# A hybrid decoder layer on one core: the first tiles' splits and square adds put on VectorE, token tile 0 reordered, attention started two sub-tiles later

## The chip, the cores and the metric

One Trainium2 chip, one of its cores. The metric is the device time of one execution of the whole program, in microseconds. Matrix products run on TensorE (PE), elementwise work on VectorE (DVE), ScalarE (ACT) and GpSimd (POOL); transfers are issued from the queues of SyncE (SP) and ScalarE. Each engine takes its instructions in program order, and the engines wait for one another by semaphores.

## What is computed

One layer, for a prompt of 1024 tokens and 8 decoding sequences of 8 tokens: 1088 tokens of 1024 channels in float32. Cut to what matters:

```python
xn = x * rsqrt(mean(x * x) + 1e-6) * g_pre
qa, ka, va, za, qm, km, vm, om, zm, ig, fg = split(xn @ w_in)
a_out = sliding_window_attention(qa, ka, va, sinks) * silu(za)   # window 128, ALiBi
h, C, n, m = mlstm(qm, km / sqrt(128), vm, ig, log_sigmoid(fg))  # chunks of 128
m_out = sigmoid(om) * rms(h, g_mh) * silu(zm)
y = concat(a_out, m_out) @ w_out
return x + rms(y, g_post), new caches, C, n, m
```

## The kernel before

Every float32 operand of a large product is split into a rounded high part and the rest, the low part, and a product is three passes: high by high, and the two mixed ones. The channels make 8 blocks, counted by kk. The 1088 tokens are cut into three sub-tiles of 368, 368 and 352 columns (SUBS); a weight tile has 128 columns of w_in, and there are 25 of them in the order ka, qa, km, qm, za, om, zm. Sub-tiles are numbered through, three to a tile: tile 5, the first of km, begins with sub-tile 15 (S_KM), and za with sub-tile 39 (S_P3).

**First tiles.** Weight tiles 0 and 1 are computed while x arrives (first_tiles, line 518). For each kk, VectorE casts the weights' high part (first_hi, 1139), GpSimd subtracts it for the low part (line 1560), ScalarE makes x's high part (862) and its square (867), and VectorE x's low part (x_lo, 1145), which PE needs for its third pass. The squares are summed in two chains: VectorE adds the odd ones (add_squares, 1154), GpSimd squares 4 and 6 into a second sum (1564), and a last add of VectorE joins the two. PE turns the sum into one column for each token tile (square_sums, 528), VectorE makes mean squares of it (1164, 1165), GpSimd raises them to the power of minus one half (1546), and PE spreads the result over partitions by nine transposes (spread_rstd, 538).

**Token tiles.** The values and gates are computed with tokens on partitions, nine tiles of 48 products each (two halves q; 324 columns), from a weight whose high part ScalarE makes in four pieces (936) and whose low part VectorE makes in four (wt_lo_part, 1159). In token tile 0 the three products of one kk stand together, each pair of blocks waits for VectorE's piece, and the transposes stand behind the fifth block. On VectorE all four pieces come before the mean squares. ScalarE copies the tile out (883), and behind it each tile of x is scaled by its rstd.

**Projections.** project() makes the other tiles, 24 products a sub-tile (590), into two PSUM banks in turn; ScalarE's evac() copies a sub-tile out (928) and, at places listed in PLAN, makes the high part of a coming weight tile (split_hi, 903); GpSimd or VectorE make the low part (split_lo, 343). Weights arrive through two buffers: load_w(n) on SP (374) waits until tile n-2 has been split. The order of SP's queue is written out by hand: loads 2 and 3, row resets, token outputs, attention biases, value bands (395, 397), two copies of old cache entries (399), loads 4 and 5, row outputs (404 to 406), and then a loop from load 6 on with the transfers of the later stages between.

**Rows and attention.** Between sub-tile 6 and 14 VectorE works out the gates' running sums and maxima as rows (1238 to 1265); PE transposes them (618) ahead of sub-tile 15, and ScalarE, behind its evacuation of sub-tile 15, takes the exponentials of these columns (967). Attention begins with sub-tile S_P2 = 16: in each iteration PE does one unit's scores (638), one sub-tile, and in every second one the values of a block (664). There are 17 units, and 23 iterations up to sub-tile 38. The first scores wait for ScalarE's exponentials (cols_done). The end of the attention gives out the keys (SP 432, 433), and only then do the first state loads (414) and weight load 14 go out; sub-tile 39 begins the mLSTM stage.

## Time and profile before

| | us |
|---|---|
| median of 3 runs | 569.39 |
| lowest and highest | 569.07, 569.61 |
| the profiled execution | 567.94 |
| its span, first to last instruction | 566.1 |
| mean granted clock of TensorE in it | 0.991 |

Times in rows count from the start of the span. In a row of the timeline the first number is the start, the second the time from the first start to the last end of the instructions merged (xN); what stands in brackets is the idle time before it and who ended it. PE's products overlap, so their durations are longer than their spacing. In the chain of waits each piece of time belongs to the work that ended last. The granted clock is a share of full speed.

### The profile page before, as it was taken

The page shows a single profiled execution, that of the slowest core. Times are in us where ns is not written, and L with a number is a line of the kernel's source. Part 1 is how long each engine was busy: PE and PEld are TensorE (multiplying, and loading weights), DVE is VectorE, ACT ScalarE, POOL GpSimd, SP SyncE. Part 2 cuts the span into 40 slices and gives each one's busy share as a digit, 9 for nine tenths or more (in the row PEclk, how much of TensorE's full clock was granted, in tenths as well). Part 3 has the DMA queues.
Part 4 walks back from the last instruction along what each step waited for, and adds up shares of the span by engine and source line. Part 5 has one row for each costly group of instructions (what it writes and reads, how often), then busy time and mean ns, then how long its engine had stood idle before and what let it go on. Part 6 is the DMA issues. An engine that isn't in the chain of part 4 may idle for free.

```text
span 566.1 us, 10430 instructions
## 1 busy us (share of the span) xinstructions
PE 550.7 (97%) x4325; PEld 507.5 (90%) x4325; DVE 281.8 (50%) x497; ACT 210.0 (37%) x538; POOL 156.7 (28%) x146
## 2 busy tenths in 40 slices
PE   8979999999799999999999999999999999999996
PEld 8979999999788989899898989899999998888874
DVE  4984655774155656530376767425333327042223
ACT  7722322341344454542565645244322234021011
POOL 2732533402132434341113131246322220011001
PEclk9989999999899999999999999999999999999998
DMA  8820000272122212113233321321123215043321
GB/s 292 301 74 2 1 1 1 62 267 75 38 75 64 86 63 63 40 38 90 69 94 112 94 75 40 93 75 38 38 75 100 87 38 186 0 164 133 108 97 56
DMA packets 36262, 48.20 MB, mean 85 GB/s; under 512 B 4128, under 2 KB 28128, under 8 KB 36200
## 3 DMA queue, kind: packets, MB, share of 16 engines
q1 hardware_dynamic: 27224, 43.15, 24.0%
q10 hardware_dynamic: 8992, 4.40, 2.8%
q8 instruction: 34, 0.56, 0.4%
q14 instruction: 12, 0.10, 0.1%
HBM read 39.96 MB, written 8.56 MB: 86 GB/s over the span
## 4 chain that ended last, share of the span: by engine, by line
PE 85%; DVE 6%; DMA 3%; issue 2%; ACT 2%; SPq 1%; POOL 1%; DVEq 0%; POOLq 0%; ACTq 0%
PE ps L590 45%; PE ps L496 8%; PE ps L497 8%; PE ps L498 8%; DVE x_hl L1145 2%; PE ps L638 2%; PE ps L664 2%; DMA w_raw<-in_w_in_tiles 2%; PE ps L738 2%; PE ps L750 1%; PE ps L714 1%; PE ps L740 1%; DMA xT_raw<-in_x_T 1%; DVE wt_lo L1159 1%; PE ps L774 1%
## 5 line engine op out<-in xcount | busy, mean ns | idle before, releaser
L590 PE MATMUL ps<-x_hl,w_hi 128*128 128x368 f32 (+1 forms) x1104 | 277.4, 332 | 0.7 <-POOL w_lo L343 0.7
L590 PEld LDWEIGHTS ps<-x_hl,w_hi 128*128 128x128 f32 x1104 | 193.9, 188 | 7.5 <-issue 5.9
L590 PE MATMUL ps<-x_hl,w_lo 128*128 128x368 f32 (+1 forms) x552 | 181.7, 329 | 0.0
L590 PEld LDWEIGHTS ps<-x_hl,w_lo 128*128 128x128 f32 x552 | 104.0, 188 | 0.1
L993 ACT ACTIVATE prob<-prob,nmx 128x160 f32<-128x160 f32 x64 | 26.6, 417 | 47.0 <-DVE sd L1298 47.0
L343 POOL TENSOR_TENSOR w_lo<-w_raw,w_hi 128x1024 fp32r<-128x1024 f32 x12 | 29.5, 2462 | 49.5 <-ACT w_hi L903 49.4
L1643 POOL TENSOR_TENSOR qmT<-qmT,sg 128x368 f32<-128x368 f32 (+1 forms) x24 | 25.0, 1042 | 57.8 <-DVE sg L1488 36.4
L496 PE MATMUL ps<-wt_hi,x_hl 128*128 128x324 f32 x128 | 40.5, 316 | 0.0
L498 PE MATMUL ps<-wt_hi,x_hl 128*128 128x324 f32 x128 | 40.4, 316 | 0.0
L497 PE MATMUL ps<-wt_lo,x_hl 128*128 128x324 f32 x128 | 40.3, 315 | 0.0
L1593 POOL TENSOR_TENSOR prob<-prob,rden 128x640 f32<-128x640 f32 x16 | 20.1, 1254 | 60.2 <-DVE rden L1304 60.2
L916 ACT ACTIVATE sg<-ps 128x368 f32<-128x368 f32 (+1 forms) x24 | 11.4, 474 | 63.6 <-PE ps L590 63.6
L1518 DVE SCALAR_TENSOR_TENSOR y_out<-ps,stat,g_post_b 128x1024 f32<-128x1024 f32 x7 | 9.0, 1284 | 49.9 <-POOL stat L1546 49.9
L1574 POOL TENSOR_TENSOR x_sc<-x_hl 128x1024 f32<-128x1024 f32 (+1 forms) x9 | 20.9, 2319 | 38.3 <-PE ps L498 36.0
L1127 ACT ACTIVATE junk<-ps 128x1024 f32<-128x1024 f32 x7 | 7.2, 1026 | 59.7 <-PE ps L498 59.7
L903 ACT ACTIVATE w_hi<-w_raw 128x1024 fp32r<-128x1024 f32 x23 | 24.2, 1051 | 7.0 <-DMA w_raw<-in_w_in_tiles 7.0
L496 PE MATMUL ps<-wah,a_hl 128*128 128x512 f32 x64 | 25.3, 395 | 0.0
L497 PE MATMUL ps<-wal,a_hl 128*128 128x512 f32 x64 | 25.3, 395 | 0.0
L498 PE MATMUL ps<-wah,a_hl 128*128 128x512 f32 x64 | 25.3, 395 | 0.0
L1650 POOL TENSOR_SCALAR stat<-stat 128x1 f32<-128x1 f32 (+1 forms) x9 | 2.3, 257 | 82.6 <-ACT junk L1127 80.7
L497 PE MATMUL ps<-wbl,m_hl 128*128 128x512 f32 x64 | 25.0, 390 | 0.0
L496 PE MATMUL ps<-wbh,m_hl 128*128 128x512 f32 x64 | 24.9, 390 | 0.0
(244 smaller groups left out, 953.3 us busy)
## 6 DMA issues: line engine op xcount, KB each, us to landing
w_raw<-in_w_in_tiles SPq DMA_DIRECT2D x23, 512.0 KB, 3.8
w_raw<-in_w_out_tiles SPq DMA_DIRECT2D x8, 512.0 KB, 3.6
x_res<-in_x_prompt SPq DMA_DIRECT2D x8, 512.0 KB, 4.2
xT_raw<-in_x_T SPq DMA_DIRECT2D x7, 544.0 KB, 8.0
out_y_prompt<-y_out SPq DMA_DIRECT2D x7, 512.0 KB, 2.9
wt_raw<-in_w_tok SPq DMA_DIRECT2D x4, 648.0 KB, 12.1
Cs<-in_state_C SPq DMA_DIRECT2D x16, 128.0 KB, 2.3
Gt<-r_rows ACTq DMA_DIRECT2D x8, 256.0 KB, 3.5
```

The costliest lines, as they stand in the source:

```text
L343: engine.tensor_tensor(lo[:, q, :], w_raw[:, n % 2, :], hi[:, q, :].bitcast(F32), ALU.subtract).then_inc(s("w_lo"), 1)
L496: mm(out, hl[:, 0, :], wh, start=first, stop=False, skip_group_check=True)
L497: mm(out, hl[:, 0, :], wl, start=False, stop=False, skip_group_check=True)
L498: return mm(out, hl[:, 1, :], wh, start=False, stop=final, skip_group_check=True)
L590: last = mm(ps[:, 6 + sub % 2, 0:w], wt, xt, start=(at_ == 0), stop=(at_ == 23))
L638: last = mm(ps[PQ * a:PQ * (a + 1), kv, g * BAND:(g + 1) * BAND], qaT[rows, 2 * pair + g, q0:q0 + PQ], kaT_pad[rows, q0:q0 + BAND], start= ...
L903: A_(dst, w_raw[:, n % 2, :], ACT.Copy).then_inc(s("w_hi"), 1)
L916: A_(sg[:, m % 2, 0:w], src, ACT.Sigmoid).then_inc(s("proj_free" if kind == "om" else "sgz_ready"), 1)
L993: A_(p, p, ACT.Exp, bias=nmx[:, b, g:g + 1], accum_out=den[:, b, g:g + 1])
L1574: Q.tensor_tensor(x_sc[:, t % 2, :, 0:n], kx(xh, off, n).bitcast(F32), kx(xl, off, n).bitcast(F32), ALU.add)\
L1593: Q.tensor_tensor(p, p, rden[:, b, :].unsqueeze(2).broadcast_to([P, G, BAND]), ALU.mult)\
L1643: Q.tensor_tensor(x, x, sg[:, m % 2, 0:w], ALU.mult).then_inc(s("sg_used"), 1)
```

## The change

Seven edits. The low parts of the first weights and all the adds of squares go to VectorE, in one chain over five buffers, and GpSimd's part of the stage is gone. The mean squares stand between the second and the third token split. Token tile 0 is ordered by kind of product: square sums, both high-weight passes of the first half, transposes, the low-weight pass, then the second half. The row transposes move behind sub-tile 15 and attention starts at sub-tile 18, so that it has 21 iterations. On SP, load 4 goes ahead of the wait for the token tiles, loads 5, 6 and 7 in among the outputs, and the cache copies behind load 7. ScalarE waits for the rows at sub-tile 15 and for the row outputs at 18, where it waited for the first of those and the transposes at 15; VectorE waits for its scaled tokens ahead of the rows. The first row tile has another place. Cut to its core:

```diff
 S_KM, S_P3, S_P4 = 3 * FIRST["km"], 3 * FIRST["za"], 3 * FIRST["om"]
-S_P2 = S_KM + 1
+S_P2 = S_KM + 3
 F_TILES = 2
...
     wt_raw = sb("wt_raw", [P, KT, TOK_W], F32, Dr + 4 * KT * TOK_W)
-    acc_2 = sb("acc_2", [P, T], F32, GI + 18688)
+    sq_b = sb("sq_b", [P, T], F32, GI + 18688)
+    sq_c = sb("sq_c", [P, T], F32, Dr + 8 * KT * TOK_W)
     x_sc = sb("x_sc", [P, 2, KT, P], F32, Dr + 8 * KT * TOK_W)
...
-    row = [sb(f"row{n}", [MH, T], F32, Dr + n * 4 * T) for n in range(6)]
+    row = [sb(f"row{n}", [MH, T], F32, Dr + n * 4 * T if n else Fr + 8 * T) for n in range(6)]
     ib, fb, ra, rb, rc, rd = row
...
-        return acc[:] if kk == 0 else acc_2[:] if kk == 2 else sq[:, kk // 2 if kk < 4 else kk % 2, :]
+        return [acc[:], sq[:, 0, :], sq[:, 1, :], sq_b[:], sq_c[:], sq[:, 0, :], sq[:, 1, :], sq_b[:]][kk]
...
         load_w(3)
+        load_w(4)
         wait(sp, "tok_done", NTILE)
...
         sp.dma_start(bias_s[:], i["bias_sample"]).then_inc(s("bias_ld"), 16)
+        load_w(5)
         sp.wait_ge(s("vrow_st"), 16)
...
         sp.dma_start(va_w[:, 1, :, :], v_band(1)).then_inc(s("vw_ld1"), 16)
-        for name, cache in (("win_k_sample", "cache_win_k"), ("win_v_sample", "cache_win_v")):
-            sp.dma_start(o[name][0, :, 0:WIN - DEC_T].rearrange("b w k d -> b (w k d)"),
-                         i[cache][0, :, DEC_T:WIN].rearrange("b w k d -> b (w k d)")).then_inc(s("out"), 16)
-        load_w(4)
-        load_w(5)
+        load_w(6)
         wait(sp, "rows_done", 1)
...
         sp.dma_start(gl_rows, r_gl[:, T_P:T]).then_inc(s("rrow_st"), 16)
+        load_w(7)
+        for name, cache in (("win_k_sample", "cache_win_k"), ("win_v_sample", "cache_win_v")):
+            sp.dma_start(o[name][0, :, 0:WIN - DEC_T].rearrange("b w k d -> b (w k d)"),
+                         i[cache][0, :, DEC_T:WIN].rearrange("b w k d -> b (w k d)")).then_inc(s("out"), 16)
...
-        for n in range(6, len(SEQ)):
+        for n in range(8, len(SEQ)):
             kind, j = SEQ[n]
...
-        def square_sums():
-            wait(pe, "acc_done", KT // 2 + 1)
-            wait(pe, "ones_ready", 1)
-            for t in range(NTILE):
-                off, n = x_cols(t)
-                last = mm(ps[0:n, 7, TOK_H + 4 + t:TOK_H + 5 + t], acc[:, off:off + n], ones[:, 0:1], start=True, stop=True)
-            last.then_inc(s("ss_cols"), 1)
+        def square_sum(t):
+            if t == 0:
+                wait(pe, "acc_done", KT - 1)
+                wait(pe, "ones_ready", 1)
+            off, n = x_cols(t)
+            last = mm(ps[0:n, 7, TOK_H + 4 + t:TOK_H + 5 + t], acc[:, off:off + n], ones[:, 0:1], start=True, stop=True)
+            if t == NTILE - 1:
+                last.then_inc(s("ss_cols"), 1)
...
         def first_token_tile():
-            for q in range(2):
-                if q == 1:
-                    wait(pe, "rstd_act", 1)
+            def product(q, kk, pas):
+                xt, wt = x_hl[:, 1 if pas == 1 else 0, kk * T:kk * T + P], wt_lo if pas == 2 else wt_hi
+                wait(pe, "wt_split_d" if pas == 2 else "wt_hi_a", kk // 2 + 1)
+                return mm(ps[:, TOK_BANK[0] + q, 0:TOK_H], xt, wt[:, kk, q * TOK_H:(q + 1) * TOK_H],
+                          start=(kk == 0 and pas == 0), stop=(kk == KT - 1 and pas == 2), skip_group_check=True)
+            for t in range(NTILE):
+                square_sum(t)
+            for pas in range(2):
                 for kk in range(KT):
-                    if q == 0 and kk == 5:
-                        spread_rstd()
-                    if q == 0:
-                        wait(pe, "wt_split_d", kk // 2 + 1)
-                    last = token_products(0, kk, q)
+                    product(0, kk, pas)
+            spread_rstd()
+            for kk in range(KT):
+                product(0, kk, 2)
+            wait(pe, "rstd_act", 1)
+            for pas in range(3):
+                for kk in range(KT):
+                    last = product(1, kk, pas)
             last.then_inc(s("tok_done"), 1)
...
         first_tiles()
-        square_sums()
         first_token_tile()
...
         last.then_inc(s("rows_ps"), 1)
-        project(24 * 8)
+        project(24 * (S_KM + 1 - S_F - 1))
         wait(pe, "rows_done", 1)
...
             .then_inc(s("cols_ps"), 1)
-        project(24 * (S_P2 - S_KM))
+        project(24 * (S_P2 - S_KM - 1))
...
         def square(kk):
-            wait(act, "acc_done", {4: 1, 5: 2, 7: 3}.get(kk, 0))
-            wait(act, "acc2_done", 1 if kk == 6 else 0)
+            wait(act, "acc_done", kk - 4)
             A_(square_at(kk), xT_raw[:, kk, :], ACT.Square).then_inc(s("sq_ready"), 1)
...
                 if sub == S_KM:
+                    wait(act, "rows_done", 1)
+                if sub == S_P2:
                     act.wait_ge(s("m_out"), 16)
+                    act.wait_ge(s("rrow_st"), 32)
                     wait(act, "cols_ps", 1)
...
+        def first_lo(kk):
+            wk = slice(kk * P, (kk + 1) * P)
+            wait(dve, "w0_hi", kk + 1)
+            TT(w_lo[:, :, wk], w_raw[:, :, wk], w_hi[:, :, wk].bitcast(F32), ALU.subtract).then_inc(s("w0_lo"), 1)
         def add_squares(kk):
-            wait(dve, "acc_done", kk // 2)
-            if kk < KT:
-                wait(dve, "sq_ready", kk + 1)
-            else:
-                wait(dve, "acc2_done", 2)
-            TT(acc[:], acc[:], square_at(kk) if kk < KT else acc_2[:], ALU.add).then_inc(s("acc_done"), 1)
+            wait(dve, "acc_done", kk - 1)
+            wait(dve, "sq_ready", kk + 1)
+            TT(acc[:], acc[:], square_at(kk), ALU.add).then_inc(s("acc_done"), 1)
...
             first_hi(kk)
+            first_lo(kk)
+            if kk >= 2:
+                add_squares(kk - 1)
             x_lo(kk)
-            if kk % 2 == 1:
-                add_squares(kk)
-        add_squares(KT)
-        for g in range(4):
-            wt_lo_part(g)
+        add_squares(KT - 1)
+        wt_lo_part(0)
+        wt_lo_part(1)
         mean_squares()
+        wt_lo_part(2)
+        wt_lo_part(3)
         first_evac()
...
         wait(dve, "rows_ps", 1)
+        wait(dve, "x_scaled", NTILE)
         for dst, bias, q in ((ib, bgi, 0), (fb, bgf, PQ)):
...
-        for kk in range(KT):
-            wait(pool, "w0_hi", kk + 1)
-            wk = slice(kk * P, (kk + 1) * P)
-            Q.tensor_tensor(w_lo[:, :, wk], w_raw[:, :, wk], w_hi[:, :, wk].bitcast(F32), ALU.subtract).then_inc(s("w0_lo"), 1)
-            if kk in (4, 6):
-                wait(pool, "sq_ready", kk + 1)
-                wait(pool, "acc2_done", kk // 2 - 2)
-                Q.tensor_tensor(acc_2[:], acc_2[:], square_at(kk), ALU.add).then_inc(s("acc2_done"), 1)
         wait(pool, "ms_ready", 1)
```

## Rows read from the trace of the kernel before

**Rows 1.** Page: its head, and part 1, busy us (share of span).
```profile
span 566.1 us, 10430 instructions
...
PE 550.7 (97%) x4325; PEld 507.5 (90%) x4325; DVE 281.8 (50%) x497; ACT 210.0 (37%) x538; POOL 156.7 (28%) x146
```

**Rows 2.** Waits of PE: who for whom, us in total, times, longest.
```profile
PE ps L638 <- issue: 3.2, 1, 3.2
...
PE ps L590 <- POOL w_lo L343: 0.7, 1, 0.7
```

**Rows 3.** Timeline of PE, 18 to 37 us: start, us, line, operation.
```profile
18.84 2.14 PE L518 MATMUL ps<-x_hl,w_hi 128*128 128x368 f32 x12
...
21.80 2.13 PE L518 MATMUL ps<-x_hl,w_hi 128*128 128x368 f32 x12
...
32.94 1.15 PE L518 MATMUL ps<-x_hl,w_hi 128*128 128x368 f32 x6
34.33 2.15 PE L528 MATMUL ps<-ones,acc 128*128 128x1 f32 x18 [0.24 <-DVE acc L1154]
```

**Rows 4.** Timeline of DVE, 10 to 40 us.
```profile
10.12 1.35 DVE L1145 SCALAR_TENSOR_TENSOR x_hl<-xT_raw,g_col,x_hl 128x1088 fp32r<-128x1088 f32 x1 [1.15 <-ACT sq L867]
11.38 1.28 DVE L1154 TENSOR_TENSOR acc<-acc,sq 128x1088 f32<-128x1088 f32 x1
12.59 0.28 DVE L1139 CAST w_hi<-w_raw 128x256 fp32r<-128x256 f32 x1
...
20.03 3.65 DVE L1145 SCALAR_TENSOR_TENSOR x_hl<-xT_raw,g_col,x_hl 128x1088 fp32r<-128x1088 f32 x1
...
34.20 5.76 DVE L1159 TENSOR_TENSOR wt_lo<-wt_raw,wt_hi 128x1296 fp32r<-128x1296 f32 x4
```

**Rows 5.** Timeline of POOL, 19 to 42 us.
```profile
19.91 2.61 POOL L1564 TENSOR_TENSOR acc<-acc,sq 128x1088 f32<-128x1088 f32 x1
...
40.16 1.82 POOL L1546 TENSOR_TENSOR stat<-stat,minus_half 128x9 f32<-128x9 f32 x1 [8.36 <-DVE stat L1165]
```

**Rows 6.** Timeline of PE, 42 to 44 us, and of ACT, 48 us.
```profile
42.04 1.28 PE L538 MATMUL ps<-ident,stat 128*128 128x128 f32 x9 [1.90 <-POOL stat L1546]
43.25 0.42 PE L496 MATMUL ps<-wt_hi,x_hl 128*128 128x324 f32 x1
...
48.49 0.69 ACT L883 ACTIVATE vm<-ps,stat 128x512 f32<-128x512 f32 x1 [4.53 <-PE ps L498]
```

**Rows 7.** Windows: length, busy us by engine, PEclk, DMA share, GB/s.
```profile
38.00:39.00 1.00, 1.00 (x5) 1.00 (x5) 1.00 (x2) 0.00 (x0) 0.00 (x0) 0.50 0.00 0
```

**Rows 8.** Timeline of POOL, 288 to 291 us, four-column instructions.
```profile
288.87 0.61 POOL L1623 TENSOR_SCALAR hf<-hf 128x4 f32<-128x4 f32 x1 [6.97 <-DVE hf L1419]
...
290.69 0.20 POOL L1625 TENSOR_TENSOR hf<-hf,hrd 128x4 f32<-128x4 f32 x1
```

**Rows 9.** Chain that ended last, by time: start us, us, what.
```profile
116.54 8.86 DMA w_raw<-in_w_in_tiles
...
149.74 1.24 PE ps L638 x32
150.98 5.33 PE ps L590 x24
...
161.02 0.70 PE ps L638 x32
161.72 4.20 PE ps L590 x24
```

**Rows 10.** Timeline of ACT, 148 and 276 us.
```profile
148.04 1.28 ACT L967 ACT_TABLE_LOAD   x1
...
276.81 1.05 ACT L903 ACTIVATE w_hi<-w_raw 128x1024 fp32r<-128x1024 f32 x1
```

**Rows 11.** Timeline of SP's DMA queue, 262 to 268 us.
```profile
262.88 4.70 SPq L374 DMA_DIRECT2D w_raw<-in_w_in_tiles  x2
```

**Rows 12.** Weight loads of line 374: time from issue to landing.
```profile
DMA to landing us min/median/max: 3.4/3.7/9.7
```

## The prediction

> **What bounds the kernel now.** I read the page first: PE is busy for 97% of the span [rows 1], so what can be won is where PE stands still or runs slowly, and the other engines matter only where PE waits for them. The waits of PE, read next, name two places behind the first stage: 3.2 us ahead of line 638 (the first scores) and 0.7 us for a weight split [rows 2]. The timeline of the first 50 us then shows a third. An undisturbed round of the first tiles takes 2.96 us (18.84 to 21.80), but the last third pass, four rounds after 18.84 and so due at 30.68, starts at 32.94: 2.26 us lost [rows 3]. VectorE's timeline says why: x_lo takes 1.35 us alone and 3.65 us at 20.03 [rows 4], where GpSimd's square add runs from 19.91 for 2.61 us [rows 5]. Behind the first tiles come the square sums (2.15 us of one-column products), held 0.24 us by VectorE's last add [rows 3], and PE then idles 1.90 us for GpSimd's power, which stood 8.36 us waiting for the mean squares [rows 5, 6]: those are queued behind all four token splits on VectorE [rows 4].
>
> **The first tiles.** GpSimd leaves them, with eight splits and two adds; VectorE gets the eight splits and two adds more (seven for five, the final merge among the five); ScalarE keeps its squares. No row has a VectorE split of 256 columns. Below it lies the cast of the same shape, 0.28 us, above it the add of 1088 columns, 1.28 us [rows 4]; its columns put it near the cast, and I take 0.4. A round on VectorE is then 0.28 + 0.4 + 1.21 (add, start to next start) + 1.26 (x_lo, likewise) = 3.15 us [rows 4]. From 11.38, where x_lo of round 1 makes way, six rounds end at 30.3; PE asks for that result at 30.68. PE stays the bound, by 0.4 us in the last round, so the 2.26 us go. At 0.6 us a split the last x_lo would come 0.8 us too late, at 1.28 us 4.9 us.
>
> **Square sums and token tile 0.** PE ends its last pass about 31.7, VectorE its last add at 31.6 (30.3 + 1.28): square sums from 31.7 instead of 34.33, over at 33.85. VectorE does two token splits of 1.44 us meanwhile (5.76 for four [rows 4]), to 34.4, and reads the mean squares by 34.65; PE waits for none of that, as it has 16 products of the first half that need only the high parts. At 0.16 us each (33 products from 43.25 to ScalarE's copy at 48.49 [rows 6]) these last to 36.4. Then comes the unknown: GpSimd's power beside VectorE's third split. Below, it takes the 1.82 us it took with VectorE at rest [rows 5]; above, it first waits out that split, 1.44 us more. The nearest row is small like it: four columns took 0.61 us where VectorE was at two-operand work, a like instruction 0.20 us later on [rows 8]. Together with the 3.65 us of x_lo I take the upper end. The Trainium skill, page "SBUF — State Buffer", section "Who interferes with whom", speaks against this placing: it has a VectorE instruction with two SBUF inputs and a GpSimd one that reads SBUF lock each other out for the whole instruction. By that rule the gain here is the 4.2 us below, without it 5.6; no row has this very pair. So the power runs from 36.05 to 37.9, the nine transposes from 37.95 to 39.15 (1.21, from 42.04 to 43.25 [rows 6]), and the other 32 products end in ScalarE's copy at 39.15 + 5.1 = 44.25 instead of 48.49: **4.2 us won**, the first tiles included. If the power doesn't wait: transposes from 36.55, copy at 42.85, 5.6 us. The fourth split, held by the power to 39.35, is there before the seventh product of its pass at 40.1; ScalarE's copy of rstd (39.8) before the second half at 40.4. Each has some 0.6 us of cover, and being late by more would cost the excess.
>
> **Tile 4's weights.** The load that held PE stood on SP behind the value-band loads and two cache copies and took 8.86 us to land [rows 9]. It is moved ahead of the wait for the token tiles, needs only tile 2's split, and lands long before its turn. **0.7 us** [rows 2]. Loads 5, 6 and 7 move up too; what they are put ahead of (band loads, row outputs) is due at the attention, tens of us later. The cache copies, moved behind load 7, are awaited only at the end. If load 5 waited long on its split, the band loads behind it would be late for the first values, which now also come two sub-tiles later.
>
> **The gate in front of attention.** Before the first scores, PE waits while ScalarE, behind sub-tile 15, splits a weight, loads a table (1.28 us from 148.04 [rows 10]) and takes the exponentials of the columns; 3.2 us [rows 2]. Then PE goes on at the lower clock: scores 1.24 us instead of 0.70, the sub-tile behind them 5.33 instead of 4.20 [rows 9], 1.7 us in sum. With the transposes now behind sub-tile 15 and sub-tiles 16 and 17 (4.2 us each) ahead of the scores, ScalarE has 8.4 us for a chain that now overhangs by 3.2. **4.9 us.** Should that cover go, 3.2 us return and with them the 1.7. ScalarE's new waits, rows ready at sub-tile 15 and row outputs stored at 18, are for events that this trace has behind it by then; behind them in its queue stand the evacuations PE needs two sub-tiles later. VectorE's new wait is for its own last instruction; the bias row only changes its place.
>
> What leaves the far end is cover: two plain sub-tiles, 8.4 us, between the last attention values and the first mLSTM step. The attention's other transfers (value bands and log weights on ScalarE's queue, sample keys on SP's) move along with it, past nothing; the key output, the first state loads and weight load 14 wait for its end. Load 14 was issued at 262.88 [rows 11] and split at 276.81 [rows 10]; in shifted time the split comes at 268.4. A usual load lands in 3.7 us [rows 12], at 266.6: covered by 1.8 us, cost nothing.
>
> **The sum.** 4.2 + 0.7 + 4.9 = 9.8 us off the profiled execution's own 567.94 us (span 566.1 [rows 1]): 558.1. The median of the runs is 569.39, 1.45 above it, so 559.6. A measurement of this kernel tells about 0.2%, 1.1 us, from no change.
>
> **The rivals.** *The power doesn't wait* (0.17): 5.6 instead of 4.2, 558.2. For it speaks that nine columns are little; against it rows 8.
>
> *The clock falls in token tile 0* (0.15). At 38 to 39 us it is granted 0.50, the 1.2 GHz level, with PE busy all that time [rows 7]; what went before was the 2.26 us lost, the wait of 0.24 and the square sums [rows 3]. The square sums stay, and 1.5 us of idling for the power follow them now. The price is that of the other fall, 1.7 us [rows 9]: 561.3. Most of a fall right behind the square sums would be hidden by the wait for the power, hence the low chance. The Trainium skill, page "TensorE: Matmul & The Clock Gate", section "What's actually happening", has the clock fall after idling and be released by activity; by that alone no fall is due here, but rows 7 show one with PE busy.
>
> *Load 14 comes late* (0.08). At the longest landing on record, 9.7 us [rows 12], it is there at 272.6, 4.2 us after ScalarE's turn; all of it would pass to PE at worst: 563.8. The long landings had cache copies in front of them, which are gone here.
>
> *The gate doesn't open* (0.05): one of ScalarE's new waits is last in place of the old chain, and 4.9 us stay, 564.5.
>
> *VectorE becomes the bound* (0.03, slower). It now does everything in the first tiles, 3.15 us a round against PE's 2.96. From 5.0 us a round (9.8 won, 1.1 to be seen and 0.4 of slack over six rounds) the kernel is slower. Were both long instructions as slow as the 3.65 us of [rows 4], a round would take 8.0 and the kernel 588 us. Against it: GpSimd, beside which that happened, has nothing to do there.
>
> **How the numbers follow.** The forecast, 559.6, has 0.50; the rest, 0.02, is for cases that cancel out within 0.2%. Faster: 0.50 + 0.17 + 0.15 + 0.08 + 0.05 = 0.95. The range goes from the first rival less 0.8 (half of the 0.54 us that the runs spread, and some 0.5 of VectorE's rounds), 557.4, to 564.5, which the closed gate gives and a split at its upper end too (559.6 + 4.9); outside lie the slow rival and the cancelling cases, 0.05, and I allow twice that for what I overlooked.
>
> **What would show it.** Right: no GpSimd work before the power; x_lo of 1.35 us throughout; the third passes 2.96 us apart to the end; square sums near 31.7; transposes at 37.95 (at 36.55 the power didn't wait), ScalarE's first token copy near 44.25; no wait of PE for w_lo line 343; scores right behind sub-tile 17 at full clock. Wrong: VectorE as releaser of the first tiles, a granted clock of 0.50 behind 36 us, PE idle near the first mLSTM scores, or ScalarE held ahead of sub-tile 18.

## The result, and the profile after

The kernel is faster, by less than half of what was forecast.

| | before | after |
|---|---|---|
| median of the runs, us | 569.33 (6 runs) | 565.13 (6 runs) |
| lowest and highest | 567.91, 569.61 | 562.14, 565.82 |
| the profiled execution | 567.94 | 565.82 |
| its span | 566.1 | 564.0 |

The ratio is 0.9915, with a 95% interval from 0.9901 to 0.993: 4.2 us won where 9.8 were forecast, and 565.1 lies 0.6 us above the range. A second measurement (e12 below) gave 564.17, ratio 0.9914 [0.9888, 0.994]. The two profiled executions differ by only 2.1 us: that of before is as short as its shortest run, that of after is the longest of its six. What follows accounts for these 2.1 us.

The waits of PE behind 30 us, in the changed kernel:

```profile
PE ps L542 <- POOL stat L1567: 2.8, 1, 2.8
PE ps L787 <- ACT ITs L1091: 1.5, 1, 1.5
PE ps L677 <- DVE pT L1331: 0.8, 1, 0.8
PE ps L651 <- DVE prob L1304: 0.4, 1, 0.4
```

The 3.2 us ahead of the first scores and the 0.7 us for tile 4's split [rows 2] are gone, as forecast. Two others have grown: the wait for the power (line 542, the transposes) is 2.8 us where it was 1.90 [rows 6], and that for ITs (787, the first mLSTM steps) is 1.5 us where it was 0.3. Two are new, 0.8 and 0.4 us within attention.

The timeline of the front, all engines (start, us, operation; in brackets the idle time before and its releaser), to be held against [rows 3 to 6]:

```profile
20.87 0.43 DVE L1166 TENSOR_TENSOR w_lo<-w_raw,w_hi 128x256 fp32r<-128x256 f32 x1
...
22.41 1.35 DVE L1160 SCALAR_TENSOR_TENSOR x_hl<-xT_raw,g_col,x_hl 128x1088 fp32r<-128x1088 f32 x1
...
34.11 2.91 DVE L1176 TENSOR_TENSOR wt_lo<-wt_raw,wt_hi 128x1296 fp32r<-128x1296 f32 x2
...
34.27 4.44 POOL L1567 TENSOR_TENSOR stat<-stat,minus_half 128x9 f32<-128x9 f32 x1 [32.52 <-DVE stat L1182]
...
30.07 0.96 PEld L521 LDWEIGHTS ps<-x_hl,w_hi 128*128 128x128 f32 x6 [0.19 <-DVE x_hl L1160]
...
31.28 2.15 PE L531 MATMUL ps<-ones,acc 128*128 128x1 f32 x18
33.36 2.63 PE L569 MATMUL ps<-wt_hi,x_hl 128*128 128x324 f32 x16
38.77 2.26 PE L542 MATMUL ps<-ident,stat 128*128 128x128 f32 x9 [2.77 <-POOL stat L1567]
...
47.98 0.69 ACT L895 ACTIVATE vm<-ps,stat 128x512 f32<-128x512 f32 x1 [6.31 <-PE ps L569]
```

VectorE's round is as worked out (split 0.43, x_lo 1.35 throughout, next start 3.13 us later), and the square sums start at 31.28 instead of 34.33. But in the last two rounds PE waits for VectorE's x_lo: its load of the stationary operand (PEld) stands 0.17 and 0.19 us, and the rounds start 3.05 and 3.13 us apart instead of 2.96. Then the power, with the same nine columns as in [rows 5], takes 4.44 us instead of 1.82; PE stands for 2.77 us and comes back at the lower clock: the transposes take 2.26 us (1.28 in [rows 6]). ScalarE's first copy is at 47.98, 0.5 us ahead of before instead of 4.2.

The windows that show the granted clock (the number behind the busy shares), in the front and at the first mLSTM steps:

```profile
38.00:39.00 1.00, 0.23 (x1) 0.24 (x2) 0.00 (x0) 0.00 (x0) 0.71 (x1) 0.76 0.00 0
40.00:41.00 1.00, 1.00 (x6) 0.55 (x4) 0.00 (x0) 0.00 (x0) 0.00 (x0) 0.50 0.09 16
45.00:46.00 1.00, 1.00 (x7) 1.00 (x6) 0.27 (x1) 0.00 (x0) 0.00 (x0) 0.82 0.00 0
...
278.00:279.00 1.00, 1.00 (x6) 1.00 (x6) 1.00 (x1) 0.13 (x1) 0.48 (x1) 0.50 0.00 0
```

It is 0.50, the 1.2 GHz level, from about 38.5 to 45.4 us (a share of the first and the last of the three windows), and again at 278; both times PE had just been standing, 2.77 and 1.51 us.

The chain of waits where attention begins:

```profile
143.84 0.78 PE ps L631 x9
144.61 0.33 PE ps L632 x2
144.94 8.07 PE ps L604 x48
153.01 0.70 PE ps L651 x32
153.71 4.21 PE ps L604 x24
...
160.45 1.52 DVE mx L1317
```

The transposes (1.11 us) stand behind sub-tile 15, two sub-tiles follow, and the scores come right behind them at full clock, 0.70 and 4.21 us against the 1.24 and 5.33 of [rows 9]. But from the next unit on the chain runs through VectorE, where a four-column instruction (line 1317) takes 1.52 us.

Attention on VectorE, three units in a row, with GpSimd's split of a weight beside the first:

```profile
177.02 2.38 POOL L344 TENSOR_TENSOR w_lo<-w_raw,w_hi 128x1024 fp32r<-128x1024 f32 x1
...
178.27 1.15 DVE L1317 TENSOR_TENSOR mx<-mx,sink_p 128x4 f32<-128x4 f32 x1
...
181.61 0.16 DVE L1324 TENSOR_TENSOR den<-den,sd 128x4 f32<-128x4 f32 x1 [1.92 <-ACT sd L1009]
...
186.88 0.16 DVE L1324 TENSOR_TENSOR den<-den,sd 128x4 f32<-128x4 f32 x1 [1.92 <-ACT sd L1009]
...
192.17 0.17 DVE L1324 TENSOR_TENSOR den<-den,sd 128x4 f32<-128x4 f32 x1 [1.92 <-ACT sd L1009]
```

From one sum of denominators (line 1324) to the next it is 5.27 and 5.29 us, but 1.0 more where line 1317 stands beside GpSimd's split of a weight, as in the unit before 181.61: there it takes 1.15 us instead of the 0.16 of the next units, and ends with the split, at 179.4. The kernel before had the same pace:

```profile
178.64 0.17 DVE L1303 TENSOR_TENSOR den<-den,sd 128x4 f32<-128x4 f32 x1 [1.92 <-ACT sd L994]
...
183.91 0.16 DVE L1303 TENSOR_TENSOR den<-den,sd 128x4 f32<-128x4 f32 x1 [1.92 <-ACT sd L994]
...
190.18 0.17 DVE L1303 TENSOR_TENSOR den<-den,sd 128x4 f32<-128x4 f32 x1 [1.92 <-ACT sd L994]
```

And its waits for PE's scores, from 150 to 250 us (in total, times, longest):

```profile
DVE prob L1283 <- PE ps L638: 9.9, 2, 8.2
```

Two of 17 units: VectorE hardly ever waited for PE there either, and hardly ever does in the changed kernel (two units again), so its chain had no room left.

The far end of attention in the changed kernel:

```profile
266.52 0.37 ACTq L1000 DMA_DIRECT2D Gt<-r_rows  x1
...
264.22 1.93 SPq L417 DMA_DIRECT2D Cs<-in_state_C  x4
266.19 0.94 SPq L375 DMA_DIRECT2D w_raw<-in_w_in_tiles  x2
...
273.50 0.69 DVE L1367 TENSOR_TENSOR DT<-Gt,causal 128x512 f32<-128x512 f32 x1 [4.01 <-DMA Gt<-r_rows]
...
276.98 0.80 PE L787 MATMUL ps<-vmk,kws 32*128 32x258 f32 x4 [1.51 <-ACT ITs L1091]
```

ScalarE issues the log weights of the first chunk (Gt, 256 KB) at 266.52, behind its evacuation of sub-tile 38; SP has just issued four state loads (264.22) and weight loads 14 and 15 (266.19). The 16 DMA engines are busy for 50% to all of the time in each us from 265 to 272. VectorE's mask, which needs Gt, waits 4.01 us for it, until 273.50: 7.0 us from issue, against a median of 3.9 for the loads of Gt in this stretch. ScalarE comes late with its exponentials, ITs is late, PE waits 1.51 us, and the clock falls.

Where the lead is won and lost is read from ScalarE's evacuations, the same instruction in both kernels (first and last start of each kind). Before:

```profile
L928 ACT ACTIVATE kmT<-ps x12: 442/454/477, 146.6 to 212.2; 128x368 f32<-128x368 f32 x8, 128x352 f32<-128x352 f32 x4
L928 ACT ACTIVATE qmT<-ps x12: 441/460/478, 217.5 to 271.2; 128x368 f32<-128x368 f32 x8, 128x352 f32<-128x352 f32 x4
L928 ACT ACTIVATE zaT<-ps x12: 463/477/478, 276.4 to 369.8; 128x368 f32<-128x368 f32 x8, 128x352 f32<-128x352 f32 x4
```

After:

```profile
L943 ACT ACTIVATE kmT<-ps x12: 443/454/478, 143.9 to 203.6; 128x368 f32<-128x368 f32 x8, 128x352 f32<-128x352 f32 x4
L943 ACT ACTIVATE qmT<-ps x12: 442/456/478, 208.9 to 266.4; 128x368 f32<-128x368 f32 x8, 128x352 f32<-128x352 f32 x4
L943 ACT ACTIVATE zaT<-ps x12: 464/477/478, 271.7 to 367.7; 128x368 f32<-128x368 f32 x8, 128x352 f32<-128x352 f32 x4
```

| lead of after, us | forecast | measured |
|---|---|---|
| first token copy | 4.2 | 0.5 |
| sub-tile 15 (first kmT), less 1.1 for the transposes that now come behind it | 4.9 | 1.6 |
| sub-tile 38 (last qmT), behind attention | 9.8 | 4.8 |
| sub-tile 50 (last zaT) | 9.8 | 2.1 |
| span | 9.8 | 2.1 |

So 3.3 us are missing when the projections reach sub-tile 15, 1.7 more are lost in attention (3.2 won instead of 4.9), and 2.7 at its far end.

### The profile page after: what moved, and what is told of

It is laid out like the page before. It is cut to its first block, busy times and chain, and to the rows that moved or that the text cites. A ratio compares the mean times of both kernels' runs of the same rounds, so it can differ in the third digit from the quotient of the medians.

```text
span 564.0 us, 10435 instructions
## 1 busy us (share of the span) xinstructions
PE 549.7 (97%) x4325; PEld 507.2 (90%) x4325; DVE 283.6 (50%) x507; ACT 209.8 (37%) x538; POOL 142.2 (25%) x136
## 4 chain that ended last, share of the span: by engine, by line
PE 72%; DVE 15%; ACT 7%; DMA 2%; issue 2%; POOL 1%; ACTq 0%; SPq 0%; DVEq 0%; POOLq 0%
PE ps L604 35%; PE ps L500 8%; PE ps L499 8%; PE ps L501 8%; ACT prob L1008 4%; DVE mx L1316 2%; DVE pT L1331 2%; DVE prob L1304 2%; DVE mx L1317 2%; PE ps L751 2%; DVE x_hl L1160 1%; DVE acc L1171 1%; PE ps L763 1%; DMA Gt<-r_rows 1%; PE ps L569 1%
## 5 line engine op out<-in xcount | busy, mean ns | idle before, releaser
L501 PE MATMUL ps<-wt_hi,x_hl 128*128 128x324 f32 x112 | 34.8, 311 | 0.0
L500 PE MATMUL ps<-wt_lo,x_hl 128*128 128x324 f32 x112 | 34.8, 311 | 0.0
L499 PE MATMUL ps<-wt_hi,x_hl 128*128 128x324 f32 x112 | 34.8, 311 | 0.0
L499 PE MATMUL ps<-wbh,m_hl 128*128 128x512 f32 x64 | 24.9, 390 | 0.0
L501 PE MATMUL ps<-wbh,m_hl 128*128 128x512 f32 x64 | 24.9, 389 | 0.0
```

The lines of the kernel that those rows point to most:

```text
L499: mm(out, hl[:, 0, :], wh, start=first, stop=False, skip_group_check=True)
L500: mm(out, hl[:, 0, :], wl, start=False, stop=False, skip_group_check=True)
L501: return mm(out, hl[:, 1, :], wh, start=False, stop=final, skip_group_check=True)
```

## The experiments

The theory: three costs of separate origin eat the gain. The power waits out both later token splits and PE's wait for it brings the clock down; attention at the pace of VectorE's chain gives back part of the gate; and with two sub-tiles of cover gone, the first log weights come late. The rivals stand with each run. Each was timed in five rounds beside the kernel before, whose medians lay between 569.27 and 569.64; the diffs show what a run adds to the changed kernel or to the run that the table names.

| run | edit | median, us | lowest, highest |
|---|---|---|---|
| e1 | root on ScalarE for the power | 560.33 | 559.06, 563.88 |
| e2 | power alone, splits behind it | 560.77 | 560.22, 563.83 |
| e3 | log weights earlier | 562.61 | 560.46, 564.07 |
| e5 | e1 and e3 | 559.03 | 557.75, 559.25 |
| e4 | attention one sub-tile later, not two | 561.00 | 559.79, 562.87 |
| e7 | e1 and e4 | 558.71 | 558.48, 559.20 |
| e6 | e1, attention in its old place | 559.67 | 559.56, 561.14 |
| e10, e13 | attention in its old place (twice) | 561.13, 563.61 | 561.05, 563.86 |
| e12 | changed kernel again, beside e13 | 564.17 | 562.45, 567.86 |
| e8 | e5, attention's splits on VectorE | 556.44 | 555.77, 558.75 |
| e9 | e7, attention's splits on VectorE | 555.90 | 555.63, 557.75 |
| e14 | e6, attention's splits on VectorE | 559.69 | 559.18, 561.13 |
| e11 | e4, PE kept busy during the power | 560.75 | 559.52, 561.00 |

**e1: no power on GpSimd.**

```diff
+        wait(act, "ms_ready", 1)
+        A_(stat[:, NTILE:2 * NTILE], stat[:, NTILE:2 * NTILE], ACT.Sqrt).then_inc(s("root_ready"), 1)
...
+        def rstd():
+            wait(dve, "root_ready", 1)
+            V.reciprocal(stat[:, NTILE:2 * NTILE], stat[:, NTILE:2 * NTILE]).then_inc(s("rstd_ready"), 1)
...
         wt_lo_part(2)
+        rstd()
         wt_lo_part(3)
...
-        wait(pool, "ms_ready", 1)
-        r = stat[:, NTILE:2 * NTILE]
-        rsqrt(r, r).then_inc(s("rstd_ready"), 1)
```

> The changed kernel with GpSimd's power taken out: ScalarE takes the square root of the nine mean squares, VectorE's reciprocal follows behind its third token split. Theory (the power waits out both later splits, and PE's wait of 2.8 us for it brings the clock down): the nine transposes begin at 36.0 to 36.3 us instead of 38.77, last 1.2 to 1.3 us, the granted clock stays at 1.0 through 38 to 45 us, ScalarE's first token copy is near 42.6 instead of 47.98, and the runs' median falls from 565.1 by 4 to 5 us, to 560 to 561. First rival (the clock falls behind the square sums whatever PE waits for): transposes at 36.0 to 36.3, but 0.50 somewhere in 34 to 45 us, copy near 44.5 to 45.5, median 562 to 563. Second rival (what is won in front is lost again in attention, where VectorE's chain sets the pace): copy near 42.6, but the lead over the kernel before at the end of sub-tile 38 stays at 4.8 us, median 564 to 565.

Its front, PE and ScalarE:

```profile
36.02 1.23 PE L542 MATMUL ps<-ident,stat 128*128 128x128 f32 x9
...
42.21 0.69 ACT L895 ACTIVATE vm<-ps,stat 128x512 f32<-128x512 f32 x1 [4.33 <-PE ps L569]
```

PE doesn't stop, the transposes run at full clock at 36.02, the copy is at 42.21, and the granted clock is 1.00 in every window from 31 to 50 us. At 560.33 it is 4.8 us under the changed kernel, as the theory said; the 1.82 us that the power takes alone go with the rest, so what it waited for is told by e2. The far end is as bad as in the changed kernel: 2.2 us of waiting for ITs.

**e2: the power alone.**

```diff
         mean_squares()
+        wait(dve, "rstd_ready", 1)
         wt_lo_part(2)
```

> The changed kernel with one wait more: VectorE holds its third and fourth token splits until the power is done. Theory (the two splits hold GpSimd off): the power lasts 1.8 us, as it did in the kernel before, instead of 4.44, from 34.3 to 36.1; the transposes begin at 36.1 to 36.3, and PE then waits 0.5 to 1 us for the fourth split (due at 39.0) in the last pass of the first half; copy of the first token tile 43.5 to 44.5, median 561 to 562. Rival (the power is slow for another reason, its first use or its place behind the memsets): it lasts 4.4 us again, transposes at 38.8, splits to 41.7, and the median is 1 to 3 us above that of the changed kernel, 566 to 568.

GpSimd's power and PE's products:

```profile
34.45 1.82 POOL L1568 TENSOR_TENSOR stat<-stat,minus_half 128x9 f32<-128x9 f32 x1 [32.70 <-DVE stat L1182]
...
33.53 4.07 PE L569 MATMUL ps<-wt_hi,x_hl 128*128 128x324 f32 x16
```

The same instruction takes 1.82 us once VectorE stands still, and 4.44 beside two splits (2.91 us in a row, which end 1.7 us before it does): that it waits for both is shown, and the median falls by 4.4 us. One thing came otherwise: the 16 products took 4.07 us instead of 2.63, because in this execution the clock fell at about 34.3, with PE busy, right behind the square sums.

**e3: the log weights ahead of the evacuation of sub-tile 38.**

```diff
+            if it == S_P3 - S_P2 - 1:
+                load_log_weights(1)
             evac(S_P2 + it)
...
-            if it + 1 <= NC:
+            if 1 <= it < NC:
                 load_log_weights(it + 1)
```

> The changed kernel with ScalarE issuing the first log-weight load (the one for chunk 1) ahead of its evacuation of sub-tile 38 instead of behind it. Theory (that load collides with state loads and two weight loads, comes 3.5 us late, and the wait of PE brings the clock down): issue near 263.1 instead of 266.5, landed before 269.5, VectorE's mask no longer waits for it, PE's wait of 1.5 us for ITs is 0.3 or less, the granted clock is 1.0 through 277 to 281 us, median 562 to 563 (2 to 3 us under 565.1). Rival (the first mLSTM steps are bound by ScalarE's work or weight load 14 instead): the mask starts earlier but PE still waits 1 us or more near 275, median within 0.7 us of 565.1.

ScalarE at the far end, and PE's waits:

```profile
271.57 1.06 ACT L915 ACTIVATE w_hi<-w_raw 128x1024 fp32r<-128x1024 f32 x1 [0.50 <-DMA w_raw<-in_w_in_tiles]
...
PE ps L787 <- ACT ITs L1093: 0.9, 1, 0.9
```

VectorE no longer waits for Gt and the clock stays up; the median is 2.5 us lower, as the theory said. PE's wait for ITs falls only to 0.9 us, because now weight load 14 is the last: ScalarE waits 0.50 us for it. The prediction's rival stands right behind the load that the prediction overlooked.

**e5: e1 and e3 together.** 

> Both edits of e1_root_dve and e3_gt_early together in the changed kernel. Theory: the two stretches have nothing to do with one another and the gains add up, 4 to 5 and 2 to 3 us: median 557.5 to 559, about the predicted 559.6 less what the missing power wins. Rival (attention's chain of VectorE and ScalarE absorbs what the front wins): no better than e3_gt_early alone by more than 1 us, 561 to 563.

559.03, 6.1 us under the changed kernel, against 4.8 and 2.5 by themselves: the costs are separate, nearly all of it adds up. No wait of PE behind 30 us is over 0.8 us (pT), and none of its five runs is more than 1.5 us from another.

**e4: one sub-tile of cover at each end.**

```diff
-S_P2 = S_KM + 3
+S_P2 = S_KM + 2
```

> The changed kernel with attention one sub-tile behind its old place instead of two (S_P2 = S_KM + 2): 4.2 us of cover in front of the scores, and one plain sub-tile more behind the last values. Theory (the far end of attention needs cover, and the gate needs only 3.2 us of it): PE waits for no ScalarE work before the first scores, the scores run at full clock, the first log-weight load lands before VectorE asks for it, PE's wait for ITs is 0.3 us, and the median is that of e3_gt_early or a little less, 561 to 563. Rival 1 (3.2 us was the part of ScalarE's chain that showed, and more of it stands behind): a wait of 0.5 us or more before the first scores, with a stretch at 0.50 behind it, 564 to 566. Rival 2 (the far end is not what costs): within 0.7 us of the changed kernel's 565.1.

```profile
PE ps L542 <- POOL stat L1567: 0.8, 1, 0.8
...
PE ps L787 <- ACT ITs L1091: 0.3, 1, 0.3
```

These are PE's waits. The gate is open and ITs costs 0.3 us, with no edit to the loads: one sub-tile does for either end. The wait for the power is 0.8 us here with the power at 4.44 us as ever: in this execution the clock fell ahead of the wait, the 16 products took 4.18 us, and the fall was hidden by the waiting. The copy is at 44.96. That is the prediction's hidden fall; the changed kernel's profile shows the exposed one, 3.0 us dearer.

**e7: e1 and e4.** 

> e1_root_dve with attention one sub-tile behind its old place (S_P2 = S_KM + 2). Theory: gate open and far end covered at once, without a change to the order of ScalarE's loads: median 557.5 to 559, as e5_root_and_gt, PE's wait for ITs 0.3 us, no stretch at 0.50 behind 100 us but the last one. Rival (gate half closed): wait before the first scores of 0.5 us or more and a fall of the clock, 560.5 to 562.

558.71, as e5 and as expected.

**e6, e10, e12, e13: attention back in its old place.** These measure the move itself.

```diff
-S_P2 = S_KM + 3
+S_P2 = S_KM + 1
```

> e1_root_dve with attention back in its old place (S_P2 = S_KM + 1), so that only the front and the weight loads of the change are left, with the power's wait taken away. Theory (the gate is worth 4.9 us and the moved attention costs 2.5 us at its far end and 1.2 to 1.7 us within): PE waits 3 us before the first scores and goes on at 0.50, the far end is covered again, and the median lies 1 to 2 us above e1_root_dve's 560.3, at 561 to 562.5. Rival (attention's chain costs nothing and the waits inside it are made up by the end): 4 to 5 us above, 564.5 to 565.5.

> The changed kernel with attention back in its old place (S_P2 = S_KM + 1), its front and its weight loads as changed: what the move of attention is worth in the change as it stands. By the difference of e6_root_shift_one and e1_root_dve (0.7 us the other way) the move is worth nothing: median 563.5 to 565.5, with a wait of 2 to 3 us before the first scores, a fall of the clock there, and none at the far end. Rival (the prediction's 4.9 us less what the far end took): 566.5 to 568.

> The changed kernel once more, beside e13 on one chip. The traces of e10_shift_one and of the changed kernel differ by 0.6 us behind sub-tile 15 (2.1 us won by the move up to the end of attention, 2.7 us lost at its far end) and by 1.6 us ahead of it, where the two programs are the same; the medians differ by 4.0 us. Theory (the move is worth about nothing, and the rest is when the clock falls in the front of a run: ahead of PE's wait for the power it is hidden, behind it it costs 1.5 to 3 us): the two kernels come out within 1.5 us of each other, both between 561 and 565, and both spread over 2 us or more. Rival (the move makes falls of the clock more frequent, or costs something that the profile of one run does not show): the changed kernel is again 3 to 4.5 us above e13.

> The kernel of e10_shift_one once more (attention in its old place, front and loads as changed). Theory: within 1.5 us of e12, 561 to 565, with spread of 2 us or more between its runs. Rival: 561 again, 3 to 4.5 us under e12.

e6 came out 0.7 us under e1: below both expectations, the move is worth nothing. e10 came out 4.0 us under the changed kernel, which neither expectation had; its evacuations say how much of that is the move:

```profile
L943 ACT ACTIVATE kmT<-ps x12: 439/455/479, 142.3 to 207.7; 128x368 f32<-128x368 f32 x8, 128x352 f32<-128x352 f32 x4
L943 ACT ACTIVATE qmT<-ps x12: 442/460/480, 212.9 to 266.9; 128x368 f32<-128x368 f32 x8, 128x352 f32<-128x352 f32 x4
L943 ACT ACTIVATE zaT<-ps x12: 464/477/478, 272.1 to 365.5; 128x368 f32<-128x368 f32 x8, 128x352 f32<-128x352 f32 x4
```

From sub-tile 15 to 38 it takes 124.6 us where the changed kernel takes 122.5; from there to sub-tile 50 it takes 98.6 against 101.3. The move wins 2.1 and loses 2.7. The other 1.6 us arise ahead of sub-tile 15, where the programs are the same. Measured side by side on one chip, the pair came out at 564.17 (e12) and 563.61 (e13): 0.6 us, as the traces say, and no more of e10's lead came back. That more of e10's runs had their fall hidden would fit; runs without a profile can't show it. In the old place PE waits 2.1 us before the scores, not 3.2: the 1.1 us of transposes, still behind sub-tile 15, fill the rest. So of the gate's 4.9 us, 1.1 belong to the place of the transposes and 3.8 to the move.

**e8, e9, e14: attention's splits on VectorE.** VectorE waits 1.92 us per unit for ScalarE's exponentials; the split goes there.

```diff
             if it < N_ATT:
                 score(it)
+            for n in PLAN.get(S_P2 + it - 1, []):
+                split_lo(dve, V, n)
...
-            splits(S_P2 + it - 1)
```

> e5_root_and_gt with attention's weight splits moved from GpSimd to VectorE, behind its scores, where it stands 1.9 us per unit waiting for ScalarE's exponentials. Theory (VectorE's chain sets attention's pace at the end because every third unit is 0.95 us longer, 6.25 instead of 5.30 us, beside a GpSimd split): all units take 5.3 us, the split of some 1.2 us is hidden, PE's waits for pT (0.8 us) and prob (0.4 us) are gone, and the median is 0.8 to 1.7 us under 559.0. Rival (the split only takes the place of the lock, and the pace stays): the third units take 6.2 us or more again, PE's waits stay, median 558.5 to 560.

> What the runs so far favour, together: the root on ScalarE in place of the power, attention one sub-tile behind its old place instead of two, and attention's weight splits on VectorE. Theory (front, far end and attention's pace are three separate costs): no PE wait for the power, none above 0.3 us before the first scores, for prob or for ITs, and weight load 14 early enough even when attention runs faster; median 556 to 557.5, and the runs closer together than the 3 us of e8_root_gt_dve_splits. Rival (with attention 1.5 us faster one sub-tile of cover is again too little at the far end): PE's wait for ITs 1 us or more, 557.5 to 559.

> e9_root_two_dve with attention in its old place (S_P2 = S_KM + 1): the move judged where VectorE's chain does not give its gain away. Theory (the gate is worth the 2.1 us of waiting and 1.7 us of clock that e6_root_shift_one shows, and only the slow pace of attention took it back): 3 to 4 us above e9's 555.9, at 558.9 to 560. Rival (attention's pace has nothing to do with it, the move is worth nothing anywhere): within 1 us of e9.

VectorE in e8, a unit with a split, and ScalarE at its far end:

```profile
184.06 0.17 DVE L1333 TENSOR_TENSOR den<-den,sd 128x4 f32<-128x4 f32 x1 [1.92 <-ACT sd L1011]
...
187.36 1.22 DVE L344 TENSOR_TENSOR w_lo<-w_raw,w_hi 128x1024 fp32r<-128x1024 f32 x1
189.36 0.16 DVE L1333 TENSOR_TENSOR den<-den,sd 128x4 f32<-128x4 f32 x1 [0.79 <-ACT sd L1011]
...
266.30 1.06 ACT L915 ACTIVATE w_hi<-w_raw 128x1024 fp32r<-128x1024 f32 x1 [1.38 <-DMA w_raw<-in_w_in_tiles]
```

The unit with the split takes 5.30 us, PE's waits for pT and prob are gone, and the median falls by 2.6 us, more than expected. From sub-tile 15 to 38 it takes 121.1 us instead of e5's 122.6, which is 1.5 of them; the profiles don't show where the rest comes from. In the execution shown, the slowest of its five, weight load 14 is 1.38 us late and PE waits 1.8 us for ITs. ScalarE's turn comes 6.0 us behind the load's issue, as in e5 (5.9), where the load was there in time; here it took 7.4 us. e9, with one sub-tile of cover, has no PE wait above 0.3 us between 30 and 400 us. PE is busy for 99% of the span; the median is 555.90, ratio to before 0.9766 [0.9741, 0.9791], the fastest version found. e14 against it is the move (by one sub-tile, which opens the gate) where VectorE's chain no longer sets the pace: 559.69 against 555.90, 3.8 us, all that the gate holds. The traces have 3.4 of it between sub-tile 15 and 38 (124.5 against 121.1 us). And e14 against e6, the same edit in the old place, wins nothing (559.69 and 559.67): behind a closed gate attention's pace costs nothing.

**e11: PE kept busy during the power.**

```diff
+            for _ in range(10):
+                mm(ps[:, 5, 368:368 + P], idle_x[:], idle_x[:], start=True, stop=True)
             spread_rstd()
```

> e4_shift_two with ten products of idle_x (128 columns, into a part of bank 5 that nothing reads before it is written) ahead of the transposes of rstd, so that PE is busy while GpSimd's power lasts; their results are never used. Theory A (PE's standing still for the power brings the clock down behind it): the transposes start at the same 38.8 us, no stretch at 0.50 follows in most runs, median 559 to 560, some 1 to 1.7 us under e4_shift_two's 561.0. Theory B (the fall goes back to the square sums and comes or not by the run, whatever PE does next): a stretch at 0.50 between 33 and 45 us as often as before, median within 0.7 us of 561.0.

The profiled execution shows no fall in the front (PE waits 0.53 us, the copy is at 44.86), but the median is 0.25 us under e4's. By the numbers set down the median speaks for the second theory and the profile for the first; five or six runs, in each of which a fall may come or not, do not tell the two apart. It stays open whether filling the wait keeps the clock up.

## Why the prediction was wrong

Three steps failed. The power's wait was sized at one split where it waited out two, and the fall of the clock behind it was left out of the sum (3.7 us together at the first token copy). The pace of attention is in no term (1.7 us). The far end was put at nothing (2.7 us).

*The first tiles: right in size, not in who came last.* Split 0.43 us for 0.4 taken, rounds of 3.13 us for 3.15; square sums at 31.28 for 31.7. But PE did not stay the bound: it waits for VectorE in the last two rounds, one of the signs set down for being wrong, at a price of 0.3 us. And the 2.26 us lost in the kernel before were not VectorE's. All three of PE's waits there, at 24.3, 27.5 and 31.9 us, were for GpSimd's low part of the weights; the longest:

```profile
31.86 1.25 PE L518 MATMUL ps<-x_hl,w_lo 128*128 128x368 f32 x6 [1.07 <-POOL w_lo L1560]
```

That split stood behind GpSimd's own square add, and VectorE's x_lo was done at 31.2. The adds and the splits left GpSimd together, so the misreading cost the forecast nothing; this was luck.

*The power: the failed step of the front.* The prediction took "the upper end", one split of 1.44 us waited out, and let the power then hold off the fourth: "from 36.05 to 37.9". It waited out both and ended at 38.71, 0.8 us later. The row it was sized by (0.61 us for four columns, [rows 8]) shows an instruction held by one other, not by a queue of them; neither bound of the range had two. The Trainium skill, page "SBUF — State Buffer", section "Who interferes with whom", says that whoever issues first keeps the shared ports for the whole instruction and the other blocks. e2 agrees as to the block (1.82 us against 4.44); here the next split of VectorE got in again ahead of the waiting power.

*The clock in token tile 0: a rival that came true, at a higher price.* It had 0.15, because "most of a fall right behind the square sums would be hidden by the wait". Both kinds exist in the runs. Hidden, or absent, the copy is at 44.86 to 45.24 (e11, e4, e13), 0.6 to 1.0 us off the forecast 44.25, which is the power's error. Behind the wait it is exposed: 46.39 (e10), 46.66 (e12), 46.84 (e3), 47.98 in the profile of after, where it lasted nearly 7 us, twice as long as in the three others. The price was taken from a fall of 1.7 us; against e4's copy it is 1.4 to 3.0. That the wait brings the clock down is not shown, though the profiles lean that way: with the power at 4.44 us and the wait for it unfilled it fell in six of six, in four of them during the wait or right behind it and in two ahead of it (e4, e13); where PE didn't stand still for the power, in four of eight (e2, e6, e7, e14).

*Tile 4 and the gate: right in themselves.* The stall is gone, the scores stand behind sub-tile 17 at full clock, and e14 against e9 shows the 3.8 us of the gate at work.

*Attention's pace: missing from the sum.* The prediction asked whether VectorE bounds the first tiles, not whether it bounds attention. Its chain needs 5.3, 5.3 and 6.3 us for three units, and in the kernel before it waited for PE in two units of 17. There PE had started attention 1.7 us late for its clock, and this hid that the chain could go no faster; with the clock restored 1.7 us were lost again (0.8 and 0.4 us of them seen on PE's list). e8 takes away the collision, and 1.5 us come back in attention; e14 against e6 shows that the collision costs nothing where the gate is closed.

*The far end: right place, wrong transfer.* "What leaves the far end is cover" was stated and costed at nothing, by looking at weight load 14 alone ("covered by 1.8 us"). The log weights "move along" with attention, "past nothing"; but for chunk 1 they are issued behind the evacuation of sub-tile 38, a fixed place, while the state and weight loads came nearer to it by two sub-tiles. That cost 2.7 us with the fall of the clock. Load 14, the rival at 0.08, is next in line (0.50 us late in e3, 1.38 in e8). It was priced at a usual landing of 3.7 us, and long landings were put down to the cache copies; with none of these near, it took 6.5 us in e3 and 7.4 in e8. The state loads that stood before it in the queue were in view and not weighed.

The sum in short, for the profiled pair: 9.8 forecast, less 3.3 up to sub-tile 15, less 1.7 in attention, less 2.7 at its far end: 2.1. Of the 3.3, 3.7 are missing at the first token copy (0.8 power, 2.9 clock), and 0.4 more than forecast come back behind it: by ScalarE's evacuations the stall of tile 4 was worth 0.9 us instead of 0.7, and the transposes 1.3 instead of 1.1.

## What to carry to other kernels

Two lists of an engine's waits belong side by side before a stall of the bound engine is priced: an engine that hardly ever waits for the bound one has no room, and takes the gain back. Cover moved from one end of a stage to the other is priced for every transfer that is due there, with its fixed place in its queue, and not only for the one that lands latest; here half the move does for both ends (e4, e7). A small GpSimd instruction on the critical path must not stand behind a run of two-input VectorE work (here 1.82 us became 4.44).

## What was not expected of the hardware

The order of waiting: nine columns of GpSimd waited for two back-to-back VectorE instructions (4.44 us instead of 1.82), while VectorE was not held at all (2.91 us for two, the pace of [rows 4]).

The clock falls with PE busy, and not by the program alone. Seven runs have the front of e1. In e1, e5, e8 and e9 the granted clock stays at 1.00 there; in e6, e7 and e14 it falls at 33.7, 34.2 and 34.2 us, behind the one-column products, with PE busy throughout (the window from 35 to 36 us in e7):

```profile
35.00:36.00 1.00, 1.00 (x5) 0.50 0.00 0
```

The Trainium skill, page "TensorE: Matmul & The Clock Gate", section "What's actually happening", has the activity watched in a rhythm of its own, which does not start with the kernel, so that the moment of a change differs from run to run. These runs agree with that: the three moments lie half a us apart. Why it falls behind busy one-column products in some runs and not in others stays open. The spread of the times goes with it in part: in e12 the run of 567.86 us had a mean granted clock of 0.983 and that of 562.45 one of 0.996, but among the runs of the result one of 563.67 us had 0.997 and one of 562.14 only 0.994.
